# The output projection's four kept weight units move into the arena, and the MLP's first two weight blocks are split before its norm loop

## What is computed

```python
mix = jnp.sum(gates * proj, axis=2) @ p['w_out']     # 640 x 1024 times 1024 x 1024
x = x + rms_norm(mix, p['norm_mix_post'])
hn = rms_norm(x, p['norm_mlp_pre'])
u = jnp.square(jax.nn.relu(hn @ p['w_up'])) @ p['w_down']
x = x + rms_norm(u, p['norm_mlp_post'])
```

## Time and profile before

| What | Value |
|---|---|
| median of 3 runs | 1533.86 us |
| profiled execution, its own time | 1532.94 us |
| its span | 1531.2 us |
| TensorE busy (matmul) | 1487.6 us, 97% |
| VectorE busy | 693.1 us, 45% |
| ScalarE busy | 616.0 us, 40% |
| mean granted TensorE clock | 0.994 of full speed |
| DMA | 143.50 MB, 94 GB/s |

### The profile page before, as it was taken

One profiled execution on the slowest core, in us unless ns is written; L12 is line 12 of the kernel. 1 busy time (PEld: TensorE's weight loads), 2 busy tenths in 40 slices (PEclk: granted clock), 3 DMA queues, 4 the chain that ended last, 5 costly groups with the idle time before them and its releaser, 6 DMA issues.

```text
span 1531.2 us, 25519 instructions
## 1 busy us (share of the span) xinstructions
PE 1487.6 (97%) x9670; PEld 1381.6 (90%) x9670; DVE 693.1 (45%) x1199; ACT 616.0 (40%) x1117; POOL 24.9 (2%) x35
## 2 busy tenths in 40 slices
PE   6899999999999999999999999999999999999996
PEld 6899999899998989998988989988998998988985
DVE  8355565532368863234444443346423323323324
ACT  6333333321267761144564542135541531531523
POOL 1000000000000000000000000000100000000003
PEclk9999999999999999999999999999999999999999
DMA  6768687322222222222432422431222222212222
GB/s 160 151 144 165 131 174 139 83 76 83 72 62 62 69 79 70 82 83 63 125 99 55 127 86 70 134 137 47 70 80 83 69 83 69 81 70 82 68 82 82
DMA packets 275213, 143.50 MB, mean 94 GB/s; under 512 B 73655, under 2 KB 260728, under 8 KB 275149
## 3 DMA queue, kind: packets, MB, share of 16 engines
q1 hardware_dynamic: 275156, 142.72, 35.0%
HBM read 129.86 MB, written 12.84 MB: 93 GB/s over the span
## 4 chain that ended last, share of the span: by engine, by line
PE 84%; DVE 6%; ACT 4%; issue 3%; DMA 1%; SPq 0%; DVEq 0%; ACTq 0%
PE psum L583 41%; PE psum L997 15%; PE psum L1031 14%; PE psum L954 2%; PE psum L769 1%; PE psum L980 1%; PE psum L680 1%; PE psum L710 1%; DMA w_raw<-in_w_in_dram 1%; ACT arena L1304 1%; PE psum L691 1%; DVE arena L1876 1%; DVE arena L1821 1%; PE psum L917 1%; PE psum L915 1%
## 5 line engine op out<-in xcount | busy, mean ns | idle before, releaser
L583 PE MATMUL psum<-XH,w_hi 128*128 128x320 f32 x1424 | 451.1, 317 | 3.1 <-ACT arena L1294 1.8
L583 PE MATMUL psum<-XH,w_lo 128*128 128x320 f32 x1424 | 440.8, 310 | 0.0
L583 PE MATMUL psum<-XL,w_hi 128*128 128x320 f32 x1424 | 440.7, 309 | 0.0
L1560 DVE TENSOR_TENSOR w_lo<-w_raw,w_hi 128x1024 fp32r<-128x1024 f32 x183 | 223.9, 1224 | 382.0 <-ACT w_hi L1132 376.2
L1132 ACT CAST w_hi<-w_raw 128x1024 fp32r<-128x1024 f32 x181 | 189.6, 1048 | 317.7 <-PE psum L1031 166.4
L583 PEld LDWEIGHTS psum<-XH,w_hi 128*128 128x128 f32 x1424 | 268.5, 189 | 15.8 <-issue 8.9
L583 PEld LDWEIGHTS psum<-XL,w_hi 128*128 128x128 f32 x1424 | 268.5, 189 | 0.6
L583 PEld LDWEIGHTS psum<-XH,w_lo 128*128 128x128 f32 x1424 | 268.1, 188 | 0.0
L997 PE MATMUL psum<-XH,w_hi 128*128 128x320 f32 x512 | 158.5, 310 | 3.2 <-DVE XL L1566 2.6
L997 PE MATMUL psum<-XH,w_lo 128*128 128x320 f32 x512 | 158.2, 309 | 0.0
L997 PE MATMUL psum<-XL,w_hi 128*128 128x320 f32 x512 | 158.2, 309 | 0.0
(11 more groups left out here) (282 smaller groups left out, 1844.8 us busy)
## 6 DMA issues: line engine op xcount, KB each, us to landing
w_raw<-in_w_in_dram SPq DMA_DIRECT2D x88, 512.0 KB, 3.7
w_raw<-in_w_up_dram SPq DMA_DIRECT2D x32, 512.0 KB, 4.0
w_raw<-in_w_down_dram SPq DMA_DIRECT2D x32, 512.0 KB, 3.5
w_raw<-in_w_branch_dram SPq DMA_DIRECT2D x24, 512.0 KB, 4.0
arena<-in_cache_fox_k_dram SPq DMA_DIRECT2D x32, 256.0 KB
arena<-in_cache_fox_v_dram SPq DMA_DIRECT2D x8, 1024.0 KB
out_dram<-arena SPq DMA_DIRECT2D x26, 256.0 KB, 2.5
arena<-in_state_gla_dram SPq DMA_DIRECT2D x4, 1024.0 KB, 5.5
```

The lines of the kernel that those rows point to most:

```text
L583: mm = pe.matmul(Z[h][:, 0:HT], w[s][:, k, :], x[:, k, h * HT:(h + 1) * HT], start=(k == 0 and i == 0), stop=(k == KT - 1 and i == 2))
L1560: dve.tensor_tensor(WL[s][:, :, :], raw[s][:, :, :], WH[s][:, :, :].bitcast(F32), ALU.subtract).then_inc(w_lo, 1)
```

## The change

A tensor `arena_r` of type float32r is laid over the same addresses as the arena, and the high and low parts of all four kept blocks get 4,096 floats each in it, at 5,120 and at 18,432. The helper views `spare` and `by_256` go. Since `w_hi` and `w_lo` are then free as soon as `out_first` has read them, M0 and M1 are copied and subtracted right behind the kept blocks, ahead of the norm loop, and no longer within its rounds 3 and 4. Every token tile takes its blocks in the order 0 to 3.

```diff
+        with nc.sbuf_tensor("arena_r", [P, ARENA], F32R) as arena_r:
+            pass
         arena = sb("arena", [P, ARENA])
...
+        W_KEEP = [[arena_r[:, at_ + n * 1024:at_ + (n + 1) * 1024].rearrange("p (k n) -> p k n", n=512) for n in range(4)]
+                  for at_ in (A0, A0 + KT * T + NT * D + 3 * D)]
+        WKH, WKL = W_KEEP
...
# TensorE, out_second(t)
-                order = (2, 3, 0, 1) if t == NT - 1 else (0, 1, 2, 3)
-                for at_, kp in enumerate(order):
+                for kp in range(KP):
...
-                    if t >= 2 and at_ == (2 if t == NT - 1 else 3):
+                    if t >= 2 and kp == (2 if t == NT - 1 else 3):
                         norm_turn(1, t - 2, HS1)
...
# ScalarE
             for kp in range(KP):
                 b = B_OUT + KP + kp
                 act.wait_ge(raw_in[b % 2], (b // 2) * 16 + 16)
-                if kp < 2:
-                    act.copy(spare(XH, kp, 0, 4), by_256(raw[b % 2])).then_inc(w_hi, 1)
-                else:
-                    act.wait_ge(z_done[1], B_OUT + kp + 1)
-                    act.copy(WH[b % 2][:, :, :], raw[b % 2][:, :, :]).then_inc(w_hi, 1)
+                act.copy(WKH[kp], RAWN[b % 2]).then_inc(w_hi, 1)
+            for n in range(2):
+                b = B_MLP + n
+                act.wait_ge(raw_in[b % 2], (b // 2) * 16 + 16)
+                act.wait_ge(z_done[1], B_OUT + 2 + n + 1)
+                act.copy(WH[b % 2][:, :, :], raw[b % 2][:, :, :]).then_inc(w_hi, 1)
 
             root_table()
...
-                if t in (NT - 2, NT - 1):
-                    hi(Lin(B_MLP + t - (NT - 2)), (B_MLP + t - (NT - 2)) % 2)
...
# VectorE
-                    lo(Lin(b), b % 2)
+                dve.tensor_tensor(WKL[kp], RAWN[b % 2], WKH[kp].bitcast(F32), ALU.subtract).then_inc(w_lo, 1)
+            for n in range(2):
+                lo(Lin(B_MLP + n), (B_MLP + n) % 2)
...
-                if t in (NT - 2, NT - 1):
-                    lo(Lin(B_MLP + t - (NT - 2)), (B_MLP + t - (NT - 2)) % 2)
```

More of the change, by code:

```diff
@@ L302, in build @@
         UBK = ((Z[0], Z[1]), (DBK[0], DBK[1]))
[L304 to L310, removed]
         def norm_bank(n, t, q):
@@ L967, in out_second @@
                     pe.wait_ge(out_free, t - 1)
-                order = (2, 3, 0, 1) if t == NT - 1 else (0, 1, 2, 3)
-                for at_, kp in enumerate(order):
+                for kp in range(KP):
                     if t == 0:
                         pe.wait_ge(w_lo, B_OUT + KP + kp + 1)
-                    if t >= 2 and at_ == (2 if t == NT - 1 else 3):
+                    if t >= 2 and kp == (2 if t == NT - 1 else 3):
                         norm_turn(1, t - 2, HS1)
                     for k in range(2):
-                        if kp < 2:
-                            wh, wl, O = spare(XH, kp, k), spare(XL, kp, k), OUTB[t].rearrange("p (a b) -> p a b", b=256)
-                        else:
[L978 to L985, removed]
+                        for i, (y, w) in enumerate(((YH, WKH), (YH, WKL), (YL, WKH))):
+                            mm = pe.matmul(OUTB[t], y[:, 2 * kp + k, tok(t)], w[kp][:, k, :], start=(kp == 0 and k == 0 and i == 0),
+                                           stop=(kp == KP - 1 and k == 1 and i == 2))
+                            if t == NT - 1 and (kp, k) == (KP - 1, 1) and i < 2:
+                                mm.then_inc(z_done[i], KP)
                 mm.then_inc(out_b, 1)
@@ L1960, in _ @@
                 b = B_OUT + KP + kp
[L1961 to L1965, removed]
-                    lo(Lin(b), b % 2)
+                dve.wait_ge(w_hi, b + 1)
+                dve.tensor_tensor(WKL[kp], RAWN[b % 2], WKH[kp].bitcast(F32), ALU.subtract).then_inc(w_lo, 1)
+            for n in range(2):
+                lo(Lin(B_MLP + n), (B_MLP + n) % 2)
             for h in range(2):
```

## The result

The changed kernel takes 1537.68 us (median of 14 runs, 1534.72 to 1538.88), the kernel before on the same chip 1533.57 (14 runs). The ratio is 1.0021, 95% interval 1.0014 to 1.0028: 3 to 4 us slower. The median lies 1.2 us above the forecast of 1536.5; since the kernel before came out 0.3 us lower than its 1533.86, the loss is 4.1 us where 2.6 were forecast. The profiled execution took 1538.36 us, span 1536.6, TensorE busy for 1491.6 us against 1487.6 before.

A forecast was written before the change was run, and what follows sets the result against it. TensorE, 97% busy, was taken to bound the kernel, so only its waits could be won. Ring delay less gains, 4.75 - 0.32 - 0.69 - 0.5 - 0.65 = +2.6 us on 1533.86, gave 1536.5 us, range 1535.3 to 1538.2.

The forecast's parts named there:

- The term that decides, M1's copy at 1045.5: ScalarE ahead of the norm loop: M1's copy waits for its load until 1045.5, so round 0 starts at 1052.3.
- Ring delay 4.75: Norm loop on ScalarE and VectorE: it begins 4.75 us late, with bounds of 4.25 and 5.05.
- The upper bound: M1's load: landing 4.3 us after issue, behind two loads in flight, would make the ring 5.05 us late.
- TensorE's stall of 3.6 us: TensorE's third token tile: it waits 3.6 us for a bank freed at 1054.95, where it never stood before.
- What comes back, 0.32 + 0.69 + 0.5 + 0.65 = 2.16: Norm rounds two to four and the last transposes: 0.32, 0.69, 0.5 and 0.65 us of the delay return.
- case A: The forecast itself: the kernel gets 2.6 us slower, 0.17%, to 1536.5 us; chance 0.5.
- B, the clock: Behind TensorE's new stall the clock halves for 3.4 us: +3.5 us, 1537.4, or 1538.2 with nothing hidden; chance 0.37.
- I price the new place at nothing: Matmuls reading kept blocks from the arena: same 24 a tile at the same pace, so no cost.
- Rival D: Something unseen, such as slower arena access: 0.01 us on each of 120 matmuls, 1.2 us more, 1537.7; chance 0.05.
- C, the ring isn't delayed, -1.9: M1's data are there when ScalarE asks at 1040.8, so only gains count: -1.9 us, 1532.0; chance 0.08.
- The border of 0.2%: Whole kernel: a difference within 0.2%, 3.07 us, counts as no change, about what a measurement can tell.
- no change that can be told: Whole kernel: a result within 0.2% of the kernel before, given 0.60, against 0.38 slower and 0.02 faster.

The follow-up runs named there:

- e6: Changed kernel with twelve unused matmuls issued where TensorE would stand still at the third token tile: 1536.43 us against 1533.61 for the kernel before, ratio 1.0015.
- e4: Changed kernel with M1's raw weights loaded earlier, into free arena room right behind M0's load: 1534.48 us against 1533.38 for the kernel before, ratio 1.0009.
- e1: Changed kernel with M1's copy and subtract moved to the end of round 0: 1533.33 us against 1533.38 for the kernel before, ratio 0.9998.
- e2: As e1, with the table load also moved ahead of M0's copy: 1532.35 us against 1533.38 for the kernel before, ratio 0.9991.
- e5: Kernel before with four unused copies on ScalarE ahead of the table load, nothing else: 1538.44 us against 1533.61 for the kernel before, ratio 1.0029.
- e3: Changed kernel with M0 and M1 back in rounds 3 and 4; M0's copy waits for the last token tile: 1538.18 us against 1533.38 before, 1.0030.
- e7: As e3, but ScalarE's wait ahead of M0 asks only that out_first is done: 1534.87 us against 1533.61 for the kernel before, ratio 1.0005.
- e11: As e2, with kept blocks 0 and 1 back in spare columns of XH and XL: 1532.64 us against 1533.22 for the kernel before, ratio 0.9997.
- e8: As e2, with the kept blocks 16 bytes further on in the arena: 1531.96 us against 1533.61 for the kernel before, ratio 0.9989.
- e9: As e2, with the kept blocks 32 bytes further on in the arena: 1532.65 us against 1533.51 for the kernel before, ratio 0.9994.

## Why the prediction was right, and where not

**The term that decides, M1's copy at 1045.5.** Right. It was forecast 4.99 us behind the start of `out_second` and stands at 5.08 (after), 5.00 (e6). Ring delay 4.75: measured 4.81 and 4.74. The upper bound had 4.3 us for a load behind two in flight, without a row for it; e4 has 4.3 and 5.3 for two close together, but in the changed kernel this load took the 4.0 of the earlier trace rows. e1 and e2 take the wait away, and the loss goes; e5 makes the delay alone, and the loss comes.

**TensorE's stall of 3.6 us.** Measured 3.18. The matmul behind the stall starts where it was forecast, 14.5 us after the start of `out_second` (14.4 forecast). TensorE came later: at 0.2333 us the 48 matmuls of the first two tiles take 0.32 us more than before, and the idle time counts from the end of the last record, 0.16 us behind the point at which the next start was due (the forecast counted from that start).

**What comes back, 0.32 + 0.69 + 0.5 + 0.65 = 2.16.** Right in sum and in its parts. e6 against the earlier trace rows by rounds: 5.82 to 5.80, 6.14 to 5.81, 6.51 to 5.80, 6.90 to 6.47; from the last reciprocal to the second halves 4.77 (1078.36 to 1083.13) before and 4.19 (1079.58 to 1083.77) now. That is 0.02, 0.33, 0.71, 0.43 and 0.58 back, 2.07 in all, and 4.74 - 2.07 = 2.67 against the +2.6 of case A. The six runs at the higher clock agree: their middle lies 2.4 us above the median of before.

**B, the clock.** The event was foreseen but put too low: it had a chance of 0.37 against A's 0.5, and eight of fourteen runs are in it. Its price was the step that failed: "Half speed for 3.4 us costs 1.7 us of work. Some 0.8 of it is hidden". The stretch at 0.50 had 5.3 us of matmuls from 1055.66 to 1061, which is 2.7 us of work; 2.1 of them reached the end (47.42 - 45.29), some 0.5 were hidden. So B stands at +4.8, not +3.5, and since more than half of the runs are in it, it sets the median. That is the 1.2 us between forecast and result, and the size of it is in part luck: with eight of fourteen runs in the slower group the median stands at that group's lower edge (1537.67 and 1537.70), and with two runs fewer in it, it would stand in the other group, near 1536.3. The length had been taken from the one fall that the earlier trace rows show, and that one does end there. It did not carry over to this place, nor to e3, where the clock was at 0.50 for some 6 us of matmuls behind a wait of 3.5 us; the other falls that the profiles hold behind waits of 1.6 to 2.7 us are as short as that of the earlier trace rows. Why the clock came back later behind the two longest, no run tells. The Trainium skill, TensorE: Matmul & The Clock Gate, section What's actually happening, tells of an array that drops to 1.2 GHz when idle and comes back with work: the trace agrees in kind, with 0.50 from about 1054 to 1061 and 1.00 behind it. But six runs of the same program have the mean of a clock that held, and stalls of 2.0 us (e4) and 2.9 us (e5) kept it in their profiles.

**"I price the new place at nothing."** Wrong. 24 matmuls at 0.0067 us more are 0.16 us a tile, 0.8 us over five. e7 shows 0.54 of it at M. In the changed kernel it is hidden, since TensorE waits for the ring there anyway, so the error did no harm to the sum. Rival D was the right kind, at 0.0067 us a matmul and not 0.01, and "No row speaks for it" holds for the trace of before, in which no matmul of this shape reads the arena.

**C, the ring isn't delayed, -1.9.** e2 makes this case: -1.17. The missing 0.7 is the arena's pace (e7, 0.54) and 0.13 less from the subtracts (1.71, not 1.84). e11, with half the blocks back in `XH`, has -1.42.

**The border of 0.2%.** The prediction gave 0.60 to "no change that can be told" and 0.38 to a slower kernel. The measured interval, 0.14 to 0.28%, lies across its border, so this doesn't decide between the two; that the kernel is slower at all is clear.

In one sum, in us of M (each term is the difference of two profiles in a row from before to after, so the terms must add up): +0.54 for the place, -1.71 for the subtracts out of rounds 3 and 4, +3.84 for M1's wait (e2 to e6, of it 0.51 for the table load behind M0's copy by e1 and e2), +2.13 for the clock: +4.80.

**A better version.** e2, e8, e9 and e11, which copy M1 in round 0 and load the table first, took 0.9989 to 0.9997 of the time before. Only e8's interval lies wholly below 1, and by 0.2% at most; by M the gain is 1.0 to 1.4 us.

## What to carry to other kernels

Work that is moved ahead of a ring to free it has to have its data there, or the engine's queue holds the whole ring up: here 1.7 us was taken out of two rounds, and a wait put in front of them that cost 3.3 (e1 against e6). Put such a copy into a gap in which the engine waits for another one anyway, as behind round 0. Price a fall of the clock by the whole stretch of matmuls that run slow, and with room for a longer one than the trace of before shows; check the pace of matmuls by their starts when an operand moves to another place.

## What was not expected of the hardware

- The moving operand's place changes the pace of a 128x512 float32r matmul: 0.2267 us from the activation or weight buffers, 0.2333 to 0.2346 us from the arena, with the start address as it was or 16, 32 or 48 bytes on, and with ScalarE and VectorE idle or at work.
- One and the same wait can keep the clock or lose it. Behind the wait of 2.6 us (L769 before) it fell in twelve of thirteen profiles, behind the 2.7 us (L954 before) in four (after, e1, e3, e8), behind the 1.6 us ahead of the second halves in one (e1).
- The longer the new stall, the more runs had a mean clock of 0.992 or less: none of 11 at 2.0 us (e4), two of 9 at 2.9 (e5), eight of 14 at 3.2 (after), seven of 8 at 3.5 (e3, at the MLP's first half blocks); with the stall filled (e6) one of 11, and of the kernel before four of the 93 runs beside the experiments. These means do not tell where a run's clock fell.
- Two loads of 512 KB that were issued 1.1 us apart took 4.3 and 5.3 us (e4), those 2 us or more apart 3.5 to 4.1 (the earlier trace rows and the profile after).
